# A hybrid scan and mixture-of-experts layer on one core: rows sorted by expert on chip, expert results put back by products

## Chip, core and metric

The kernel runs on one core of one Trainium2 chip. The metric is the device time of one execution in microseconds, as the median of three runs.

## What is computed

One layer of a diffusion trunk on 384 tokens (128 prompt, 256 sample) of width 1024, all in float32: a modulated norm, a wide projection, two groups of scans (Mamba-2 and RWKV-7), the output product, and then the part that the change is about, a mixture of 32 experts of which each token uses two:

```python
h = rmsnorm(x, norm2_w) * (1.0 + scale2) + shift2
grp_logits = (t @ w_grp) + b_grp                  # 4 groups, the best one is taken
exp_logits = (t @ w_exp) + b_exp                  # 8 experts in it, the best two
gates = sum(one_hot(expert_id) * top_w)           # two weights of each token
hid = silu(einsum('td,edf->tef', t, w_gate)) * einsum('td,edf->tef', t, w_up)
out = einsum('tef,efd->td', hid * gates, w_down)  # D = 1024, D_EXPERT = 256
x = x + gate2 * out
```

A last norm follows, and the outputs are stored.

## The kernel before, in words

The kernel is written engine by engine, with semaphores set by hand; each engine runs its list in order. `ps` is PSUM with 8 banks of 512 columns; `P` = 128, `NTILE` = 3 token tiles, `T` = 384, `KT` = 8 channel tiles.

**First pair.** While TensorE runs the 27 projection tiles (`project`, L1641, in a loop over t), VectorE mixes each tile as it comes (`mix`, L2306) and prepares the arrays of the first pair of RWKV heads between them: part 4 of `prep_dve` (L926, L927) behind the mix of tile 24, part 5 (L931, L932) behind that of tile 25. TensorE transposes their result (L494) behind the projection of tile 25. POOL clears two stretches of a ring (L1545) behind `proj_read` of the last tile.

**Router.** After the mix product (L1876), VectorE adds the three tiles of x1, ScalarE computes their roots, TensorE transposes all three (L1888), VectorE makes `hT` out of it in 16 pieces (L2484), one product of 36 rows gives the logits (L1893), they are transposed back (L1897), and VectorE picks the experts (from L2503) and hands the assignments to TensorE for the ranks in each expert (L1908, L1911). `keep_warm` (L453) puts small matmuls between.

**Groups.** Each expert has a chunk of `CH` = 64 slots, and a group is two chunks, so 16 groups (`NG`), and one to five overflow groups for experts with more than 64 tokens; with these inputs there is one. For group n VectorE builds a 0/1 matrix `pick` (`select`, L1253 to L1265), TensorE gathers the tokens of the group by 24 matmuls with it (`rows_T`, L1218), VectorE copies them (L1272), and TensorE forms gate and up for both experts at once in two column tiles of 64 (`gate_up`, L1229). ScalarE applies silu, VectorE multiplies, TensorE transposes the hidden rows (`hidden_T`, L1238), VectorE copies (L1284), TensorE forms the down product in column tiles (`down_proj`, L1249), and ScalarE copies it (`expert_out`, L1296) and stores it to DRAM (`y_dram`). On TensorE the order of a group is gate/up of n, hidden transposes of n-1, gathering of n+1, down product of n-1:

```python
gate_up(pe, n, b)
if not first:
    hidden_T(pe, n - 1, 1 - b)
rows_T(pe, n + 1)
if not first:
    down_proj(pe, n - 1, 1 - b)
```

SP loads the weights of two groups ahead (`expert_gate_up`, `expert_down`), 6.29 MB for a group.

**End.** POOL gathers for each token the two rows of `y_dram` that are its own (six indirect DMAs, L1582), ScalarE and VectorE weigh and add them (`x2_tile`, L2586 to L2596), and the last norm and the stores follow (L2601, L1448).

Of the kernel before, what the change touches and what calls it, by code (L numbers as in the profile page):

```python
# [15 lines left out]
ds = bass.ds  # L16
# [86 lines left out]
def program(nc, a, out):  # L103
    ctx = ExitStack()
    with ctx:
# [853 lines left out]
        def round_dve(dve, c, b, prev, nxt):  # L959
# [97 lines left out]
            if prev:  # L1057
# [9 lines left out]
        xgT = at(um_f, 2048, 2, KT, P)  # L1067
        yg = at(um_f, 4096, 2, D)
        hs = at(um_f, 6144, 2, DE)
        hid = at(um_f, 6656, 2, DE)  # L1070
        hidT = at(um_f, 7168, 2, 2, P)
        wr = at(um_f, 7680, KT, 36)
        h2sq = at(um_f, 4096, D)
        mx_f = mixm[:, :, :].rearrange("p i t -> p (i t)")
        fnw = at(mx_f, 0, D)
        ymoe = misc[:, 10240:10240 + D]
        lg = at(scratch, 0, NTILE, 36)
        lgT = scratch[0:36, 2048:2048 + T]
# [10 lines left out]
        irow = at(scratch, 880, P)  # L1089
        srel = at(scratch, 872, 2, NTILE)  # L1090
        pick = at(scratch, 2432, NTILE, P)
        erow = at(scratch, 1011, 32)
        down = at(scratch, 1043, 36)
        brt = at(scratch, 1079, 36)
# [7 lines left out]
        slots_i = wdt_f[:, 0:6].bitcast(U32)  # L1102
        gcol = wdt_f[:, 112:144].rearrange("p (t v) -> p t v", v=2)
        meta_i = wdt_f[:, 150:151 + N_CHUNKS + N_OV].bitcast(I32)
        zrow = vrows[0:16, 0, :]
        cmb = at(um_f, 0, 2, 2, D)
        rconst = sem("zeros_and_router_constants")
# [4 lines left out]
               [[(at(misc, 3072, 2, 4, DE), 0, 4), (at(um_f, 0, 2, 4, DE), 4, 4)],  # L1112
                [(at(mx_f, D, 2, 4, DE), 0, 4), (at(misc, 10240, 2, 4, DE), 4, 4)]]]
        wdn = [[at(h, 4096, 2, D) for h in half], [at(hT_flat, 0, 2, D), at(um_f, 7968, 2, D)]]
        GU_LOADS, DN_LOADS = (4, 8), 2
# [8 lines left out]
        y_dram = nc.dram_tensor("expert_rows", [N_GROUPS * P, D], F32).ap()  # L1124
# [16 lines left out]
        lgT_ok = sem("expert_major_logits_ready")  # L1141
# [3 lines left out]
        slots_ok = sem("slots_ready")  # L1145
        meta_ok = sem("loop_table_ready")
        zero_ok = sem("overflow_rows_zeroed")
        sel_c = sem("selection_steps")
        sel_ok = sem("selection_ready")
        gu_in = [sem("gate_up_loaded_0"), sem("gate_up_loaded_1")]  # L1150
        dn_in = [sem("down_loaded_0"), sem("down_loaded_1")]
        yst = [sem("expert_rows_stored_0"), sem("expert_rows_stored_1")]
        xt_ps = sem("rows_transposed")
        xt_rd = sem("rows_ready")
# [7 lines left out]
        comb = [sem("combined_rows_0"), sem("combined_rows_1")]  # L1162
        moe_ok = sem("moe_summed")
        cmb_w = sem("first_expert_row_weighed")
# [46 lines left out]
        def rows_T(pe, n):  # L1211

            pe.wait_ge(sel_ok, n + 1)
            if late(n, 1):
                pe.wait_ge(xt_rd, n)
            for k in range(KT):
# [3 lines left out]
            mm.then_inc(xt_ps, 1)  # L1220

        def gate_up(pe, n, b, before=2):
            pe.wait_ge(xt_rd, n + 1)
            if late(n, 2):
                pe.wait_ge(hid_ok, n - (before - 1))
            for k in range(KT):
                for x in range(2):
                    h = slice(CH * x, CH * x + CH)
                    mm = pe.matmul(ps[h, 2 + b, :], xgT[:, b, k, h], gate_up_tile(b, x, k), start=(k == 0),  # L1229
                                   stop=(k == KT - 1), tile_position=(0, CH * x), skip_group_check=True)  # L1230
            mm.then_inc(gu_ps, 1)
# [21 lines left out]
        def select(dve, n):  # L1253

            if late(n, 1):
                dve.tensor_scalar(srel, srel, float(P), None, ALU.subtract).then_inc(sel_c, 1)
            else:
                dve.tensor_copy(srel, slots).then_inc(sel_c, 1)
            dve.wait_ge(sel_c, n * 2 + 1)
            for j in range(NTILE):  # L1260
                ins = dve.tensor_scalar(pick[:, j, :], irow, srel[:, 0, j:j + 1], None, ALU.is_equal)
            ins.then_inc(sel_c, 1)
            dve.wait_ge(sel_c, n * 2 + 2)
            for j in range(NTILE):
                ins = dve.scalar_tensor_tensor(pick[:, j, :], irow, srel[:, 1, j:j + 1], pick[:, j, :], ALU.is_equal, ALU.add)  # L1265
# [1369 lines left out]
```

## Time and profile before

| what | us |
|---|---|
| median of 3 runs (1238.7 to 1243.1) | 1241.46 |
| the profiled execution's own time | 1237.3 |
| its span | 1235.4 |
| TensorE matmul busy, share of the span | 1128.7 (91%) |
| VectorE busy | 562.6 (46%) |
| ScalarE busy | 333.8 (27%) |
| GpSimd busy | 139.4 (11%) |
| mean granted TensorE clock | 0.955 |

All durations of the trace are from the one profiled execution. Its rows name engines PE (TensorE matmul), PEld (weight load), DVE (VectorE), ACT (ScalarE), POOL (GpSimd), SPq (the sync engine's queue), and source lines as L1229. PEclk is the granted TensorE clock as a share of 2.4 GHz; 0.50 is 1.2 GHz. In a chain, each piece is the work that released the next one; in a timeline, the brackets tell how long the engine sat idle and what ended it.

### The profile page before, as it was taken

The numbers are of one execution on the slowest core, as the hardware profiler recorded it, in microseconds if no ns is written. First come the engines' busy times: TensorE is split into PE (matmuls) and PEld (weight loads), VectorE is DVE, ScalarE is ACT, GpSimd is POOL, SyncE is SP. The second block draws the span as 40 slices with busy tenths as digits, with TensorE's granted clock in tenths as the row PEclk, the third lists the DMA queues.
The fourth block names the chain that finished last, engine by engine and source line by source line (L and its number), as shares of the span: only waits on it lengthen the run. The fifth ranks groups of instructions, "written<-read, shape, count | busy, mean of one in ns | idle before, by whom it ended". The sixth has DMA issues, their size and how long they took to land.

```text
span 1235.4 us, 34632 instructions
## 1 busy us (share of the span) xinstructions
PE 1128.7 (91%) x15658; PEld 722.3 (58%) x15658; DVE 562.6 (46%) x1305; ACT 333.8 (27%) x701; POOL 139.4 (11%) x186
## 2 busy tenths in 40 slices
PE   5899889999999779999999999789989999999990
PEld 3555336677765466656666566575575555555540
DVE  0355102567676465756657666531662212222214
ACT  2022101322234244535445345321220000000012
POOL 6000001032103030303203023000000000000002
PEclk9899988999999889999999999879999999999995
DMA  9533555331218201110211201203286999999874
GB/s 333 205 136 136 204 204 160 103 86 68 69 30 129 45 4 33 56 55 27 73 43 44 64 28 37 105 3 103 71 360 235 408 416 416 416 416 415 334 287 159
DMA packets 83665, 201.28 MB, mean 163 GB/s; under 512 B 12484, under 2 KB 27079, under 8 KB 78919
## 3 DMA queue, kind: packets, MB, share of 16 engines
q1 hardware_dynamic: 79392, 186.97, 42.2%
q10 hardware_dynamic: 3271, 9.08, 1.8%
q0 software_dynamic: 864, 3.15, 0.8%
q8 instruction: 116, 1.90, 0.6%
q14 instruction: 22, 0.18, 0.0%
HBM read 183.97 MB, written 15.20 MB: 161 GB/s over the span
## 4 chain that ended last, share of the span: by engine, by line
PE 86%; DVE 4%; DMA 3%; issue 3%; ACT 3%; POOL 0%; POOLq 0%; SPq 0%; ACTq 0%; DVEq 0%; PEldq 0%
PE ps L1641 16%; PE ps L1229 10%; PE ps L1218 7%; PE ps L568 5%; PE ps L1249 5%; PE ps L616 4%; PE ps L1684 4%; PE ps L1876 3%; PE ps L550 2%; PE ps L1764 2%; PE ps L1780 2%; PE ps L482 2%; PE ps L600 1%; DMA ring_a<-in_w_in 1%; PE ps L1603 1%
## 5 line engine op out<-in xcount | busy, mean ns | idle before, releaser
L1641 PE MATMUL ps<-hT,ring_a 128*128 128x384 f32 x624 | 215.7, 501 | 3.4 <-DVE hT L2224 2.5
L1641 PEld LDWEIGHTS ps<-hT,ring_a 128*128 128x128 f32 x624 | 119.7, 196 | 85.1 <-issue 9.5
L1218 PE MATMUL ps<-scratch,misc 128*128 128x128 f32 x864 | 99.7, 275 | 1.3 <-DVE scratch L1265 1.3
L1218 PEld LDWEIGHTS ps<-scratch,misc 128*128 128x128 f32 x864 | 97.9, 192 | 3.1 <-issue 3.1
L2306 DVE SCALAR_TENSOR_TENSOR um_a<-ps,mum,um_a 128x252 f32<-128x252 f32 (+1 forms) x162 | 57.3, 410 | 73.2 <-ACT um_a L2023 72.2
L568 PEld LDWEIGHTS ps<-ring_a 32*32 32x32 f32 x6144 | 63.0, 106 | 42.8 <-issue 30.2
L568 PE MATMUL ps<-ring_a 32*32 32x32 f32 x6144 | 71.6, 195 | 14.9 <-issue 14.9
L1229 PE MATMUL ps<-ring_a,um_a 128*64 128x512 f32 x288 | 63.4, 593 | 1.6 <-DVE um_a L1272 1.4
L1284 DVE COPY um_a<-ps 128x256 f32<-128x256 f32 x17 | 7.2, 425 | 125.5 <-PE ps L1238 125.5
L1508 POOL TENSOR_TENSOR mixm<-tri,la 128x512 f32<-128x512 f32 x24 | 28.4, 1207 | 271.8 <-DVE la L2276 187.2
L1229 PE MATMUL ps<-misc,um_a 128*64 128x512 f32 x128 | 56.3, 592 | 1.4 <-DVE um_a L1272 1.4
L1296 ACT ACTIVATE um_a<-ps 128x1024 f32<-128x1024 f32 x17 | 17.4, 1026 | 143.0 <-PE ps L1249 143.0
L616 PE MATMUL ps<-ring_a,mixm 128*128 128x512 f32 x96 | 54.0, 645 | 0.0
L1272 DVE COPY um_a<-ps 128x1024 f32<-128x1024 f32 x17 | 20.8, 1225 | 71.5 <-PE ps L1218 70.7
L1684 PE MATMUL ps<-ring_a,hT 128*128 128x512 f32 x96 | 46.8, 648 | 6.9 <-DMA ring_a<-in_w_in 6.9
L2023 ACT ACTIVATE um_a<-ps,mum 128x384 f32<-128x384 f32 x27 | 15.7, 582 | 130.6 <-PE ps L1641 130.6
L1582 POOL DMA_INDIRECT um_a<-expert_rows,wdt x6 | 6.7, 1122 | 367.9 <-DMA expert_rows<-um_a 361.9
L1229 PEld LDWEIGHTS ps<-ring_a,um_a 128*64 128x64 f32 x288 | 21.1, 137 | 42.0 <-issue 42.0
L999 DVE COPY_PREDICATED ring_a<-lvl,ps 128x128 f32<-128x128 int32 x96 | 26.7, 278 | 39.4 <-PE ps L568 39.1
L1603 PE MATMUL ps<-ring_a,cond 128*32 128x512 f32 x192 | 28.2, 712 | 12.7 <-DMA ring_a<-in_w_ada 10.3
L1290 ACT ACTIVATE um_a<-ps 128x256 f32<-128x256 f32 x17 | 6.5, 385 | 122.0 <-PE ps L1229 122.0
L1684 PEld LDWEIGHTS ps<-ring_a,hT 128*128 128x128 f32 x96 | 19.6, 208 | 31.1 <-issue 24.0
(422 smaller groups left out, 2009.0 us busy)
## 6 DMA issues: line engine op xcount, KB each, us to landing
ring_a<-in_w_ada SPq DMA_DIRECT2D x12, 2048.0 KB, 12.5
ring_a<-in_w_in SPq DMA_DIRECT2D x11, 2048.0 KB, 9.1
ring_a<-in_moe_w_gate SPq DMA_DIRECT2D x18, 1024.0 KB, 9.4
ring_a<-in_moe_w_up SPq DMA_DIRECT2D x18, 1024.0 KB, 11.6
ring_a<-in_moe_w_down SPq DMA_DIRECT2D x18, 1024.0 KB, 11.8
ring_a<-in_w_out SPq DMA_DIRECT2D x48, 256.0 KB, 2.7
expert_rows<-um_a ACTq DMA_DIRECT2D x17, 512.0 KB, 7.0
misc<-in_moe_w_gate SPq DMA_DIRECT2D x16, 512.0 KB, 9.2
```

Of the source, the lines that this page charges most:

```text
L568: mm = pe.matmul(ps[r, 2 * s + 1, m:m + 32], lhs[r, h, d, :], rhs[r, h, d, :], start=True, stop=True, tile_position=(32 * q, 32 * q), skip ...
L616: pe.matmul(ps[:, 7, :], mixm[:, k, P * (r // 2):P * (r // 2) + P], mamba_w[n % RING], start=(k == 0), stop=(k == KT - 1)).then_inc(half_p ...
L999: dve.copy_predicated(xc[s], level_mask(l, False), ps[:, 2 * s + 1, P:2 * P].rearrange("p (h d q) -> p h d q", h=2, d=2)).then_inc(x_ok, 1)
L1218: mm = pe.matmul(ps[:, k // 4, P * (k % 4):P * (k % 4) + P], h2[:, j, P * k:P * k + P], pick[:, j, :], start=(j == 0), stop=(j == NTILE - 1))
L1229: mm = pe.matmul(ps[h, 2 + b, :], xgT[:, b, k, h], gate_up_tile(b, x, k), start=(k == 0), stop=(k == KT - 1), tile_position=(0, CH * x), s ...
L1249: mm = pe.matmul(ps[h, 5 + c, :], hidT[:, b, k, h], wdn[b][x][:, k, BLK * c:BLK * c + BLK], start=(k == 0), stop=(k == 1), tile_position=( ...
L1508: ins = pool.tensor_tensor(lam[:, j, 4 * d:4 * d + 4, :], tri[:, 2 - 2 * d, :].unsqueeze(1).to_broadcast([P, 4, P]), la[:, j, h:h + 4].uns ...
L1603: mm = pe.matmul(ps[32 * q:32 * q + 32, ada_bank(i), :], cond[:, 2 * q + k2, :], slot(n)[:, 2 * q + k2, :], start=(k2 == 0), stop=(k2 == 1 ...
L1641: mm = pe.matmul(ps[:, t % 4 if isinstance(t, int) else t, 0:T], slot(n)[:, k, P * c:P * c + P], hT[:, k, :], start=(k == 0), stop=(k == K ...
L1684: mm = pe.matmul(ps[:, i % 4, :], hT[:, k, P * j:P * j + P], slot(n)[:, k, :], start=(k == 0), stop=(k == KT - 1))
L1876: mm = pe.matmul(ps[:, 2 * j + c, :], um_a[:, k, P * j:P * j + P], wout_tile(k)[:, BLK * c:BLK * c + BLK], start=(k == 0), stop=(k == KT - 1))
L2306: ins = dve.scalar_tensor_tensor(dst, src, mum[:, m, t:t + 1], dst, ALU.mult, ALU.add)
```

## The change

It does four things. (1) The first pair's parts 4 and 5 on VectorE move one tile ahead, and POOL's memsets wait for the projection in place of its reading. (2) The router goes by token tiles: transposes, halves of `hT` on VectorE and ScalarE, and logits for each tile, with the tokens on the rows of the result; its weights are loaded ahead of x. (3) `rows_T` in each group goes. Once, before the first group, `sort_rows` puts all 768 token rows in the order of their experts, channel-major in `sortT`, by products with a 0/1 matrix `pk`; for each group VectorE reads two offsets into registers and copies two stretches of 64 columns (`expert_columns`). (4) The expert rows are no longer stored to DRAM and gathered. A matrix `put` that holds each token's weight at its slot is built for each group (`put_matrix`), and six matmuls (`put_unit`: three token tiles by two halves) give the group's share of all 384 tokens, which VectorE adds up in `acc2` (`add_units`). In the loop the units of group n-2 stand between the gate/up products of group n. `acc2` is weighed and added to x1 ahead of the overflow group, whose units are added one by one. TensorE's loop is written out instead of run by registers; one gate/up weight block is in three pieces instead of two.

The diff, cut to its core ("..." marks what is left out):

```diff
@@ L1211, rows gathered per group -> rows sorted once; units
-        def rows_T(pe, n):
...
+        def sort_rows(pe):
+            for i in range(2 * KT):
+                blk, k = i // KT, i % KT
+                if k == 0:
+                    pe.wait_ge(pk_ok, blk + 1)
+                if i >= 6:
+                    pe.wait_ge(srt_sb, i - 5)
                 for j in range(NTILE):
-                    mm = pe.matmul(ps[:, k // 4, P * (k % 4):P * (k % 4) + P], h2[:, j, P * k:P * k + P], pick[:, j, :],
+                    mm = pe.matmul(ps[:, i % 6, 0:T], h2[:, j, P * k:P * k + P], pk[blk][j],
                                    start=(j == 0), stop=(j == NTILE - 1))
+                mm.then_inc(srt_ps, 1)
+        def slot_rows(pe):
+            pe.wait_ge(slots_ok, 1)
+            for i, cols in enumerate((slots[:, 0], slots[:, 1], wcol[:, 0], wcol[:, 1])):
+                for j in range(NTILE):
+                    mm = pe.matmul(ps[:, (0, 1, 5, 6)[i], P * j:P * j + P], cols[:, j:j + 1].to_broadcast([P, P]), ident[:, :],
+                                   start=True, stop=True)
+            mm.then_inc(row_ps, 1)
+        UNIT_BANK = (0, 1, 7)
+        def put_unit(pe, m, b, u):
+            if u == 0:
+                pe.wait_ge(put_ok, m + 1)
+                pe.wait_ge(yg_ok, m + 1)
+            if late(m * 6 + u, 3):
+                pe.wait_ge(unit_rd, m * 6 + (u - 2))
+            pe.matmul(ps[:, UNIT_BANK[u % 3], :], put[b][:, P * (u // 2):P * (u // 2) + P],
+                      yg[:, BLK * (u % 2):BLK * (u % 2) + BLK], start=True, stop=True).then_inc(unit_ps, 1)
@@ gate_up: the units of group n - 2 behind k = 1 to 6
-            pe.wait_ge(xt_rd, n + 1)
+            pe.wait_ge(x_in, n + 1)
...
+                if behind is not None and 1 <= k < 7:
+                    put_unit(pe, behind, behind % 2, k - 1)
@@ L1253, VectorE's helpers: select and rows_copy go
+        def expert_columns(dve, n, b, chunks, before=2):
+            rows = [dve.value_load(off_i[0:1, ds(c, 1)], min_val=0, max_val=2 * T) for c in chunks]
             if late(n, 2):
                 dve.wait_ge(gu_ps, n - (before - 1))
+            dve.tensor_copy(xgT[b][:, :, 0:CH], sortT[:, :, ds(rows[0], CH)])
+            dve.tensor_copy(xgT[b][:, :, CH:P], sortT[:, :, ds(rows[1], CH)]).then_inc(x_in, 1)
+        def put_matrix(dve, m, b):
...
+            dve.scalar_tensor_tensor(put[b], slot_row[:, 0, :], prow[:, 0:1], w_row[:, 0, :], ALU.is_equal, ALU.mult)
+            dve.scalar_tensor_tensor(put_k, slot_row[:, 1, :], prow[:, 0:1], w_row[:, 1, :], ALU.is_equal, ALU.mult).then_inc(put_c, 1)
+            dve.wait_ge(put_c, m * 2 + 2)
+            dve.tensor_tensor(put[b], put[b], put_k, ALU.add).then_inc(put_ok, 1)
+        def add_units(dve, m):
+            for u in range(6):
+                dst, src = acc2[:, u // 2, BLK * (u % 2):BLK * (u % 2) + BLK], ps[:, UNIT_BANK[u % 3], :]
+                dve.wait_ge(unit_ps, m * 6 + u + 1)
+                if m:
+                    dve.wait_ge(unit_rd, m * 6 + u - 5)
+                    dve.tensor_tensor(dst, dst, src, ALU.add).then_inc(unit_rd, 1)
...
@@ L1292, expert_out: no store to DRAM
+            if late(m, 1):
+                act.wait_ge(unit_ps, m * 6)
+            act.activation(yg.rearrange("p (c n) -> p c n", c=2), ps[:, 5:7, :], ACT.Copy).then_inc(yg_ok, 1)
-            act.dma_start(y_dram[ds(m * P, P), :], yg[:, b, :]).then_inc(yst[b], 16)
@@ POOL: memsets of the first pair; the gathers go
-            pool.wait_ge(proj_read, XBC + 6 + RT)
+            pool.wait_ge(proj, XBC + 6 + RT)
...
-                    pool.indirect_dma_start(out=cmb[:, j % 2, k, :], out_offset=None, in_=y_dram,
@@ L1882, TensorE: router by tiles, then the loop, unrolled
+            x1_T(0)
+            keep_warm(pe, ps[:, 6, 0:P], 4)
+            x1_T(1)
+            keep_warm(pe, ps[:, 6, 0:P], 4)
+            pe.wait_ge(late_in, 16 * 4)
+            logits(0)
+            logits(1)
+            h2_back(0)
+            x1_T(2)
+            keep_warm(pe, ps[:, 6, 0:P], 8)
+            logits(2).then_inc(lg_ps, 1)
+            h2_back(1)
+            h2_back(2)
...
+            sort_rows(pe)
+            for n in range(NG):
+                i, b = n // 2, n % 2
+                pe.wait_ge(gu_in[b], (i + 1) * (16 * GU_LOADS[b]))
+                gate_up(pe, n, b, behind=n - 2 if n >= 2 else None)
+                if n == 0:
+                    slot_rows(pe)
+                else:
+                    hidden_T(pe, n - 1, 1 - b)
+                    pe.wait_ge(dn_in[1 - b], (n + 1) // 2 * (16 * DN_LOADS))
+                    if n == 1:
+                        pe.wait_ge(row_ok, 1)
+                    down_proj(pe, n - 1, 1 - b)
             hidden_T(pe, NG - 1, 1)
+            for u in range(6):
+                put_unit(pe, NG - 2, 0, u)
             pe.wait_ge(dn_in[1], NG // 2 * (16 * DN_LOADS))
             down_proj(pe, NG - 1, 1)
+            for u in range(6):
+                put_unit(pe, NG - 1, 1, u)
             with pe.Fori(0, overflow(pe)) as o:
...
-                rows_T(pe, o + (NG + 1))
+                for u in range(6):
+                    put_unit(pe, o + NG, 0, u)
@@ L2432, VectorE: the first pair's parts one tile sooner
-                elif t == 24:
+                elif t == 23:
                     dve.wait_ge(yT_ps, 8)
                     prep_dve(dve, -1, 0, pc, 4)
-                elif t == 25:
+                elif t == 24:
                     prep_dve(dve, -1, 0, pc, 5)
@@ VectorE: the sorting matrix
+            for blk in range(2):
+                for j in range(NTILE):
+                    ins = dve.tensor_scalar(pk[blk][j], iw[:, blk, :], pos[:, 0, j:j + 1], None, ALU.is_equal)
+                chain.do(ins)
+                for j in range(NTILE):
+                    ins = dve.scalar_tensor_tensor(pk[blk][j], iw[:, blk, :], pos[:, 1, j:j + 1], pk[blk][j], ALU.is_equal, ALU.add)
+                ins.then_inc(pk_ok, 1)
@@ VectorE: the loop and what follows
+            for n in range(1, NG):
+                if n >= 2:
+                    add_units(dve, n - 2)
+                hidden_copy(dve, n - 1, 1 - n % 2)
+                hidden_mul(dve, n, n % 2)
+                if n < NG - 1:
+                    expert_columns(dve, n + 1, 1 - n % 2, (2 * n + 2, 2 * n + 3))
+                put_matrix(dve, n - 1, 1 - n % 2)
+            hidden_copy(dve, NG - 1, 1)
+            put_matrix(dve, NG - 1, 1)
+            add_units(dve, NG - 2)
+            add_units(dve, NG - 1)
...
+            for j in range(NTILE):
+                ins = dve.tensor_tensor(acc2[:, j, :], acc2[:, j, :], g2[:, min(j, 1), :], ALU.mult)
+            chain.do(ins)
+            for j in range(NTILE):
+                ins = dve.tensor_tensor(x1[:, j, :], x1[:, j, :], acc2[:, j, :], ALU.add)
+            chain.do(ins)
             with dve.Fori(0, overflow(dve)) as o:
+                expert_columns(dve, o + NG, 0, (o * 2 + 2 * NG, o * 2 + (2 * NG + 1)), before=1)
+                put_matrix(dve, o + NG, 0)
                 hidden_mul(dve, o + NG, 0, before=1)
                 hidden_copy(dve, o + NG, 0, before=1)
+                for u in range(6):
...
+                    dve.tensor_tensor(acc2[:, j, c], ps[:, UNIT_BANK[u % 3], :], g2[:, min(j, 1), c], ALU.mult).then_inc(unit_rd, 1)
+                    dve.wait_ge(unit_rd, (o + NG) * 6 + u + 1)
+                    dve.tensor_tensor(x1[:, j, c], x1[:, j, c], acc2[:, j, c], ALU.add).then_inc(put_add, 1)
```

## Rows read from the trace of the kernel before

**Rows 1.** Page, part 4: share of the chain that ended last, by engine.
```profile
PE 86%; DVE 4%; DMA 3%; issue 3%; ACT 3%; POOL 0%; POOLq 0%; SPq 0%; ACTq 0%; DVEq 0%; PEldq 0%
```

**Rows 2.** Chain, third group and one steady group: start us, us, engine, tile, line, count.
```profile
957.18 6.87 PE ps L1229 x32
...
1005.72 6.87 PE ps L1229 x32
1012.59 0.37 PE ps L1238 x2
1012.95 5.36 PE ps L1218 x48
1018.31 3.58 PE ps L1249 x16
```

**Rows 3.** Windows: busy us (instructions) of PE, PEld, DVE, ACT, POOL; PEclk, DMA share, GB/s.
```profile
850.00:860.00 10.00, 10.00 (x38) 5.53 (x37) 0.00 (x0) 1.02 (x1) 0.00 (x0) 1.00 0.00 0
...
1090.00:1100.00 10.00, 10.00 (x72) 6.84 (x70) 1.50 (x3) 0.39 (x1) 0.00 (x0) 1.00 1.03 418
...
1208.00:1212.00 4.00, 0.00 (x0) 0.00 (x0) 0.00 (x0) 0.00 (x0) 3.09 (x4) 0.68 0.64 184
```

**Rows 4.** Timeline around the last projections of the first pair: start us, us, engine, line.
```profile
400.80 10.59 PE L1641 MATMUL ps<-hT,ring_a 128*128 128x384 f32 x32 [0.90 <-DVE um_a L2306]
...
415.21 1.08 PE L494 MATMUL ps<-ident,misc 128*128 128x128 f32 x4 [3.82 <-DVE misc L931]
...
416.09 7.73 PE L1641 MATMUL ps<-hT,ring_a 128*128 128x384 f32 x16
```

**Rows 5.** Timeline from the mix product's end to the ranks.
```profile
885.64 5.52 PE L453 MATMUL ps<-ident 128*128 128x128 f32 x48
...
904.17 0.27 DVE L2503 TENSOR_TENSOR scratch<-ps,scratch 128x108 f32<-128x108 f32 x1 [6.39 <-PE ps L1897]
...
909.89 0.41 PE L1908 MATMUL ps<-scratch,tri 128*128 128x32 f32 x2
...
911.25 0.83 PE L1911 MATMUL ps<-scratch,ones 128*128 128x32 f32 x6
```

**Rows 6.** Timeline, passes of 384 columns: ScalarE out of PSUM, VectorE in SBUF.
```profile
394.77 0.49 ACT L780 ACTIVATE pair<-ps 128x384 f32<-128x384 f32 x1
...
919.97 0.55 DVE L2557 TENSOR_TENSOR scratch<-scratch 128x384 f32<-128x384 f32 x1
```

**Rows 7.** Timeline, VectorE at the entry of the overflow loop.
```profile
1185.32 1.23 DVE L1272 COPY um_a<-ps 128x1024 f32<-128x1024 f32 x1 [0.79 <-issue]
```

**Rows 8.** Chain, mix product, matmuls of 512 columns.
```profile
868.63 17.17 PE ps L1876 x40
```

**Rows 9.** Chain, the overflow group: hidden transposes and down products.
```profile
1196.83 0.44 PE ps L1238 x2
...
1197.83 3.67 PE ps L1249 x16
```

**Rows 10.** Timeline of one group, edges between tiled and full-array products.
```profile
1011.99 0.59 PE L1229 MATMUL ps<-um_a 128*64 128x512 f32 x1
...
1012.52 0.44 PE L1238 MATMUL ps<-ident,um_a 128*128 128x128 f32 x2
...
1012.79 5.52 PE L1218 MATMUL ps<-scratch,misc 128*128 128x128 f32 x48
...
1018.24 3.65 PE L1249 MATMUL ps<-ring_a,um_a 128*64 128x512 f32 x16
...
1021.73 7.04 PE L1229 MATMUL ps<-ring_a,um_a 128*64 128x512 f32 x32
```

**Rows 11.** Timeline of the end: last square on ScalarE, last table load, last scale.
```profile
1220.51 1.28 ACT L2183 ACT_TABLE_LOAD   x1
...
1229.35 1.06 ACT L2181 ACTIVATE um_a<-misc 128x1024 f32<-128x1024 f32 x1 [2.60 <-DVE misc L2596]
...
1231.06 1.28 DVE L2601 SCALAR_TENSOR_TENSOR misc<-misc,mstat,mixm 128x1024 f32<-128x1024 f32 x1
```

More of the change, by code:

```diff
@@ L1251, in down_proj @@
             mm.then_inc(dn_ps, 1)
[L1253 to L1265, printed above, removed]
-            ins.then_inc(sel_ok, 1)
@@ L2520, in _ @@
             dve.tensor_tensor(s3[:, 4, :], s3[:, 3, :], s3[:, 2, :], ALU.subtract).then_inc(rt_dve, 1)
+            dve.wait_ge(lg_ps, 2)
+            n_e = ps[:, 7, 96:128]
+            rank = ps[:, 7, 0:96].rearrange("p (j e) -> p j e", j=NTILE)
+            chain.do(dve.tensor_tensor_scan(n_to, ones[:, 0:32], n_e, 0.0, ALU.mult, ALU.add))
+            chain.do(dve.tensor_tensor(first, n_to, n_e, ALU.subtract))
+            chain.do(dve.tensor_tensor(slot_v, rank, row(first, 32), ALU.add))
+            for k in range(2):
+                chain.do(dve.tensor_tensor(tmp, slot_v, oh[:, k], ALU.mult))
+                chain.do(dve.tensor_reduce(pos[:, k, :], tmp, AX.X, ALU.add))
+            for blk in range(2):
[5 more added lines that the diff above has]
+                ins.then_inc(pk_ok, 1)
+            dve.tensor_copy(off_i[:, 0:NE], first).then_inc(meta_ok, 1)
             dve.wait_ge(rt_act, 1)
@@ L2558, in _ @@
             chain.do(dve.tensor_tensor(mq, mq, mq2, ALU.mult))
+            chain.do(dve.scalar_tensor_tensor(off_m, cnt[:, 2, :], -float(CH), first, ALU.mult, ALU.add))
+            chain.do(dve.tensor_tensor(mq2, mq, by_chunk(off_m), ALU.mult))
+            chain.do(dve.tensor_reduce(off_x, mq2, AX.X, ALU.add))
+            chain.do(dve.scalar_tensor_tensor(off_x, erow[:, 0:n_ov], float(CH), off_x, ALU.mult, ALU.add))
+            chain.do(dve.tensor_reduce(s_q, mq, AX.X, ALU.max))
+            chain.do(dve.scalar_tensor_tensor(off_x, s_q, float(CH), off_x, ALU.mult, ALU.add))
+            dve.tensor_copy(off_i[:, NE:N_CHUNKS], off_x)
             chain.do(dve.tensor_tensor(mq, mq, by_chunk(erow), ALU.mult))
@@ L2568, in _ @@
             dve.tensor_copy(meta_i[:, :], meta).then_inc(meta_ok, 1)
[L2570 to L2574 removed]
+            dve.wait_ge(meta_ok, 2)
+            dve.wait_ge(rconst, 2)
+            dve.wait_ge(srt_sb, 2 * KT)
+            expert_columns(dve, 0, 0, (0, 1))
+            expert_columns(dve, 1, 1, (2, 3))
+            dve.wait_ge(row_ps, 1)
+            for i in range(2):
+                dve.tensor_copy(slot_row[:, i, :], ps[:, i, 0:T])
+                ins = dve.tensor_copy(w_row[:, i, :], ps[:, 5 + i, 0:T])
```

318 lines of the change are left out of this document (142 added, 176 removed).

## The prediction

> **What bounds the kernel now.** Read the chain of waits on the page first: TensorE carries 86% of it [rows 1]. Then the chain through the expert groups: one group is 6.87 + 0.37 + 5.36 + 3.58 = 16.18 us of gate/up products, hidden transposes, row gathering (`rows_T`) and down products, with nothing between them, and the pattern stands 14 times, from 957.18 to 1183.7 [rows 2]. The windows show the transfers close beside it: DMA share 1.03 at 418 GB/s [rows 3]. A group reads 6.29 MB and stores 0.52 MB, so 6.81/16.18 = 421 GB/s: TensorE sets the pace and the transfers just keep up. So only TensorE's work in a group counts in the loop; outside it, the waits do.
>
> The parts are costed in order of time, against the profiled execution: 1235.4 us span, 1237.3 us time.
>
> **First pair, -6.** TensorE stood idle 3.82 us for VectorE's L931, which came behind the mix of tile 25; the next 16 matmuls then took 7.73 us, where 32 take 10.59, so 5.3 is their price at full clock, and the difference is 2.4 [rows 4]. One tile earlier, L931 stands behind the mix of tile 24 and ends about when that of tile 25 began, so TensorE finds it done. Gain 3.8 + 2.4 = 6.2; ends: nothing (another input is late in its place) and 6.7 (the transposes too run at full clock). I take 6. POOL's memsets behind `proj` instead of `proj_read`: nothing, VectorE's own chain to L2442 releases the same products. The router's four loads move ahead of x's two on SP: nothing, the transfers stand still from 850 to 860 and VectorE, which x feeds, works in none of these 10 us [rows 3].
>
> **From the mix product to the third group, +12.5.** The product ends at 885.8 in both; before, the router began at 904.17 [rows 5]. By tiles: VectorE adds the last x1 tile as before (two passes of 1.23, to 888.4), a root and the first half-tile follow on ScalarE, so `logits(0)` can start near 891.0. From there TensorE runs in order 80 small instructions (logits 3x16, transposes 8+8, warm 16) at 0.12 each (48 took 5.52 [rows 5]), 9.6 us: 900.6, a gain of 3.6. To the assignments 5.7 and the ranks 2.2 as before [rows 5]: 908.5. New on VectorE: seven small steps (about 1.9) and the first block of the sorting matrix, six passes of 384 columns; one took 0.55 [rows 6], and compares should be somewhat faster: 2.9. At 913.3 TensorE starts `sort_rows`: 2 x 8 x 3 matmuls of 384 columns, each two instructions in float32 as in `project`, 96 x 0.331 [rows 4] = 31.8 us, all of it bare, since the first group needs all 16 results; ScalarE's copies (0.49 [rows 6]) hide but the last. End 945.6. Then `expert_columns`: two register loads and two copies of 512 elements. Before, one load with the loop's entry kept VectorE idle 0.79 us [rows 7]; I take 0.8 each, and 0.5 per copy (ends 0.4 and 0.7: no row copies within the chip at this size). First gate/up at 948.4; it takes 7.1, then slot rows 24 x 0.112 = 2.7, gate/up 6.9, transposes with their wait 1.1, down 3.5: third group at 969.7 against 957.2.
>
> **Fourteen groups, +26.2.** `rows_T` goes (5.36). Six put units come: each one float32 matmul of 512 columns, two instructions at 17.17/40 = 0.429 [rows 8], 5.15 together. That alone would gain 0.2. Two things are added. (a) The hidden transposes now stand directly ahead of the down products, with nothing to cover VectorE's copy between. The overflow group of before already runs so: transposes at 1196.83, down at 1197.83 [rows 9]. 1.00 where the steady group pays 0.37: +0.6. (b) A unit uses the whole array, gate/up and down use it as two column tiles of 64. Tiled pairs follow each other at 0.43; behind the last pair (1011.99) the full-array transpose starts 0.53 later, so 0.10 is lost; from the first of the 48 gathers (1012.79) to the first tiled pair (1018.24) are 5.45 against 5.36 in the chain, 0.09 lost, and its eight pairs need 3.49 against 3.44, 0.05 [rows 10]. A round trip costs 0.24 us, six stand in every group: 1.44 us.
> The Trainium skill (TensorEngine Tiling (Array Packing), Key Properties) says that changing the tiling mode, not just the tile, drains TensorE. It speaks against the interleaving; if the drain is what the recorded 0.59 us of a matmul has over its 0.43 spacing, 0.16 each way, the sum by it would be 14 x 6 x 0.08 = 7 us longer; my sum goes by the spacing in the rows.
> New group: 6.87 + 5.15 + 1.44 + 0.10 + 1.00 + 3.49 = 18.05, +1.87, times 14 = 26.2. The switch may cost 0 to 0.32, that is -20 to +7. What hides: VectorE adds the units, six of about 0.7 (half and a little of 1.23 for 1024 elements [rows 7]), while they come every 1.9 us, so three banks do; ScalarE's copy of the down result ends 1.1 us behind it, the first unit comes at 1.7. `expert_out` now waits for the units of the group before, which are long done, and behind it on ScalarE only the next silu stands. Columns of the next group: behind the transposes 0.9 (copy, multiply) + 1.6 + 1.0 = 3.5 us, against 4.4 until TensorE asks; if that cover is gone each us costs 14. Transfers fall to 6.29/18.05 = 348 GB/s; the two more weight pieces per odd group cost SP 0.9 us of issue in its idle time.
>
> **End of the loop to the last down product, +25.5.** Before 1183.7 to 1201.5 = 17.8 [rows 2, 9]. After, in a row: units of group 14 with a wait of 1.2 for ScalarE's copy and 5.15, down 3.6, copy 1.2, units of group 15 5.15, last add 0.8: 17.1. Then VectorE weighs and adds acc2 in six passes of 1024, 6 x 1.23 = 7.4, and only behind them come loop entry 0.8, loads 1.6, copies 1.0 and a hand-over 0.1 for the overflow group, which always runs once: 28.0. TensorE has idled 11 us by then. Before, its last matmul ended near 1207, and the granted clock of 1208 to 1212 was 0.68 [rows 3]: the group begins at half clock, and as in rows 4 some 2.5 us are added to 7.1. Then silu and product 1.0, transposes 1.1, down 3.6: 43.3.
>
> **Tail, -12.6.** Before 1201.5 to 1235.4 = 33.9: store, six gathers from DRAM, sums, norm. After: copy and first unit 2.3; VectorE multiplies, then adds, each of six half rows, 12 x 0.7 = 8.5; square to scale 1.7 and a table load 1.3 for the first tile, 1.5 for each other; from the last scale (1231.06) to the end 4.3 [rows 11]: 21.3 with 0.2 of hand-overs.
>
> Sum: -6 + 12.5 + 26.2 + 25.5 - 12.6 = +45.6, so 1282.9. The median of the runs shown, 1241.5, lies 4.2 above the profiled execution; with it 1287.1. I put 1285.
>
> **Rivals.** (1) *Switches cost nothing* where a unit of 0.86 us follows, since its second weights load early. For: the losses of rows 10 are at small matmuls. Against: they stand at both kinds of edge. -20: 1265. Chance 0.2.
> (2) *VectorE becomes the bound.* Its place is `expert_columns`; it decides from 0.9 us more than my 3.5. For: 0.79 idle for one load [rows 7], and no row shows such a copy. At 1 us late per group +14: 1299. Chance 0.15. The Trainium skill (DMA: Bandwidth & Descriptors, Latency and other measured facts) gives some 600 ns as the least for a `tensor_load`; two would be 1.2 us by it, and the columns would not be late.
> (3) *Faster than before.* The one mechanism big enough: put units run beside the tiled products, TensorE taking both in little more than the time of one. The units are 84 in the loop at 1.10 and 18 behind it at 0.86, 108 us; the gain begins once one costs under about 0.63 us, less than its own two passes. Free units leave the groups at the transfers' floor (6.29/421 = 14.9 us, -17 in place of +26) and take 10 off the end: 1232. Against: rows 8 show 0.429 for each pass with the array to itself, and a steady group has no idle TensorE time. Chance 0.05.
> (4) *The early preparation does not do what it says*, another input is late: +6, 1291. Chance 0.1.
> The forecast has 0.5.
>
> **Numbers.** Under about 0.3% (4 us) a measurement of this kernel can't tell a change from none. Rival 3 and a little of 1 with other errors on the same side are faster or same: faster 0.05, same 0.02, slower 0.93. Range 1258 to 1304: free switches and 7 us more that I overcharged, to late columns and a half clock behind the sort as well.
>
> **What would show it.** Groups of 18.05 us in the chain, put units between tiled pairs; `sort_rows` as 31 us of TensorE; TensorE idle about 11 us before the overflow group; no 3.8 us idle before the transposes near 411. Wrong if a group is near 16.6 (free switches), if VectorE's columns release gate/up, or if the time falls below 1258.

## The result, and the profile after

The changed kernel takes 1296.2 us (median of 4 runs, 1289.4 to 1300.9), the kernel before 1240.1 in the same comparison: ratio 1.046, 95% interval [1.0423, 1.0497]. Forecast were 1285, a range of 1258 to 1304, and slower with a chance of 0.93. The profiled execution of after took 1300.9 us (span 1299.2), 4.7 more than its median; that of before lies 2.8 below its own. So the spans differ by 63.8 us, the medians by 56.

The page of the changed kernel, busy times (part 1) and the chain by engine (part 4), which stands at 86% for TensorE in [rows 1]:

```profile
PE 1191.5 (92%) x15131; PEld 684.8 (53%) x15131; DVE 631.7 (49%) x1395; ACT 342.5 (26%) x725; POOL 134.5 (10%) x181
...
PE 88%; DVE 4%; issue 3%; DMA 3%; ACT 1%; DVEq 0%; SPq 0%; PEldq 0%; ACTq 0%
```

TensorE is the bound before and after, and the span grew by 63.8 us while its busy time grew by 62.8. Where they came, cut at the same four points in both profiled executions:

| stretch | before | after | difference | forecast |
|---|---|---|---|---|
| start to the mix product's end | 885.8 | 882.3 | -3.5 | -6 |
| to the third group's gate/up | 71.4 | 91.3 | +19.9 | +12.5 |
| fourteen groups | 226.5 | 261.7 | +35.2 | +26.2 |
| end of the loop to the last down product | 17.8 | 42.8 | +25.0 | +25.5 |
| tail | 33.9 | 21.1 | -12.8 | -12.6 |

One steady group in the chain of waits (start us, us, engine, line, count), to be held against [rows 2]:

```profile
973.59 1.72 PE ps L1266 x8
975.31 1.06 PE ps L1256 x2
976.36 1.01 PE ps L1266 x4
977.37 1.06 PE ps L1256 x2
...
987.70 0.37 PE ps L1278 x2
988.07 0.56 issue
988.63 3.65 PE ps L1289 x16
992.28 0.82 PE ps L1266 x3
```

L1256 is a put unit, L1266 gate/up. The group is 992.28 - 973.59 = 18.69 us. A unit and the four gate/up instructions behind it take 2.07; the passes alone are 2 x 0.429 + 4 x 0.215 = 1.72. So one round trip between the two tilings costs 0.35 us, where 0.24 were forecast. The timeline shows its edges (start us, us, engine, line, shapes):

```profile
1217.71 0.59 PE L1266 MATMUL ps<-mixm,hT 128*64 128x512 f32 x1
1218.23 1.12 PE L1256 MATMUL ps<-mixm,scratch 128*128 128x512 f32 x2
1219.29 0.64 PE L1266 MATMUL ps<-misc,hT 128*64 128x512 f32 x1
...
1219.77 0.59 PE L1266 MATMUL ps<-misc,hT 128*64 128x512 f32 x1
```

Tiled pairs follow each other at 0.43. Into the unit it is 0.52 (0.10 lost, as in [rows 10]); the unit's two passes are worth 0.86 and the next tiled pair comes 1.06 behind its start (0.20 lost, where [rows 10] gave 0.09 behind a small matmul); the next pair comes 0.48 later (0.05 lost). Every product has a weight load (PEld) on record, and these loads tell where the time goes:

```profile
1217.24 0.14 PEld L1266 LDWEIGHTS ps<-misc,hT 128*64 128x64 f32 x1 [0.26 <-issue]
...
1218.23 0.30 PEld L1256 LDWEIGHTS ps<-mixm,scratch 128*128 128x128 f32 x2 [0.81 <-issue]
1219.28 0.13 PEld L1266 LDWEIGHTS ps<-misc,hT 128*64 128x64 f32 x1 [0.76 <-issue]
```

Between tiled products the weights are loaded one product ahead: the load of 1217.24 belongs to the product that starts at 1217.67. At a change they are not: both loads of the unit start with its first product at 1218.23, and the load of the tile behind it starts at 1219.28.

Behind the mix product, TensorE's timeline (in brackets the idle time before, and what ended it) and the windows (busy us of PE, PEld, DVE, ACT, POOL; PEclk, DMA share, GB/s) of the changed kernel:

```profile
884.74 1.06 PE L453 MATMUL ps<-ident 128*128 128x128 f32 x8
887.84 6.24 PE L1929 MATMUL ps<-um_a,hT 128*128 128x36 f32 x32 [2.04 <-ACT hT L2196]
...
907.51 0.41 PE L1956 MATMUL ps<-scratch,tri 128*128 128x32 f32 x2 [0.85 <-DVE scratch L2573]
```
```profile
888.00:892.00 4.00, 4.00 (x24) 4.00 (x23) 0.20 (x1) 1.09 (x4) 0.00 (x0) 0.59 1.02 428
892.00:896.00 4.00, 4.00 (x20) 4.00 (x21) 0.00 (x0) 0.00 (x0) 0.00 (x0) 0.50 1.00 411
896.00:900.00 4.00, 4.00 (x26) 4.00 (x25) 1.36 (x4) 2.43 (x5) 0.00 (x0) 0.63 1.02 410
```

The logits of two tiles (L1929) took 6.24 us at half clock, and the ranks' products start 25.4 us behind the first instruction that follows the mix product, where before it was 24.3. VectorE's passes for the sorting matrix and its last table entry, and the sort in the chain:

```profile
913.14 1.67 DVE L2590 SCALAR_TENSOR_TENSOR um_a<-rst,scratch,um_a 128x384 f32<-128x384 f32 x3
...
929.42 0.19 DVE L2643 CAST wdt<-scratch 128x51 int32<-128x51 f32 x1
950.91 0.43 DVE L1298 COPY states<-um_a 128x512 f32 x1 [21.30 <-issue]
```
```profile
910.06 7.60 PE ps L453 x56
917.66 30.98 PE ps L1234 x96
```

The first block of the sorting matrix is ready at 914.8, but the sort starts at 917.7: released by the 56 warming instructions ahead of it. The sort is 30.98 us, and VectorE's last table entry is done at 929.6. TensorE has nothing beside the sort, and the chain goes through all of it. But the table stands ahead of the first columns in VectorE's list, so a shorter sort would save at most the 19.0 us from 929.6 to 948.6; the first 12 run beside the table.

The end, in the chain. TensorE stands still from 1252 to 1263:

```profile
1246.58 5.40 PE ps L1256 x12
...
1252.80 3.51 DVE misc L2672 x3
1256.36 1.10 issue
1257.47 2.36 DVE misc L2675 x2
...
1263.14 9.29 PE ps L1266 x32
...
1274.43 3.67 PE ps L1289 x16
```

### The profile page after: what moved, and what is told of

It reads as the page before. It is cut to its first block, busy times and chain, and to the rows that moved or that the text cites. A ratio compares the mean times of both kernels' runs of the same rounds, so it can differ in the third digit from the quotient of the medians.

```text
span 1299.2 us, 33869 instructions
## 1 busy us (share of the span) xinstructions
PE 1191.5 (92%) x15131; PEld 684.8 (53%) x15131; DVE 631.7 (49%) x1395; ACT 342.5 (26%) x725; POOL 134.5 (10%) x181
## 4 chain that ended last, share of the span: by engine, by line
PE 88%; DVE 4%; issue 3%; DMA 3%; ACT 1%; DVEq 0%; SPq 0%; PEldq 0%; ACTq 0%
PE ps L1677 15%; PE ps L1266 10%; PE ps L1256 8%; PE ps L568 5%; PE ps L1289 5%; PE ps L616 4%; PE ps L1720 4%; PE ps L1912 3%; PE ps L1234 2%; PE ps L550 2%; PE ps L1800 2%; PE ps L1816 2%; PE ps L482 1%; PE ps L600 1%; DMA ring_a<-in_w_in 1%
## 5 line engine op out<-in xcount | busy, mean ns | idle before, releaser
L1321 DVE TENSOR_TENSOR misc<-misc,ps 128x512 f32<-128x512 f32 x90 | 61.8, 688 | 133.1 <-PE ps L1256 133.0
L1266 PE MATMUL ps<-ring_a,states 128*64 128x512 f32 x288 | 75.1, 624 | 14.5 <-DVE states L1299 14.5
L1266 PE MATMUL ps<-misc,hT 128*64 128x512 f32 x128 | 65.3, 609 | 0.0
L1256 PE MATMUL ps<-mixm,stw 128*128 128x512 f32 x108 | 58.3, 635 | 2.2 <-ACT mixm L1347 1.4
L1256 PE MATMUL ps<-mixm,scratch 128*128 128x512 f32 x96 | 52.7, 639 | 1.2 <-issue 1.2
L1266 PEld LDWEIGHTS ps<-ring_a,states 128*64 128x64 f32 x288 | 18.5, 139 | 64.2 <-issue 64.2
L1639 PE MATMUL ps<-ring_a,cond 128*32 128x512 f32 x192 | 28.1, 710 | 12.6 <-DMA ring_a<-in_w_ada 10.1
L1256 PEld LDWEIGHTS ps<-mixm,stw 128*128 128x128 f32 x108 | 16.8, 188 | 42.5 <-DVE misc L1321 24.8
L971 DVE TENSOR_TENSOR ring_a<-ps,tri 128x512 f32<-128x512 f32 x48 | 30.6, 679 | 16.3 <-PE ps L550 16.3
L1347 ACT ACTIVATE mixm<-ps 128x1024 f32<-128x1024 f32 x17 | 17.4, 1024 | 77.3 <-PE ps L1289 77.3
## 6 DMA issues: line engine op xcount, KB each, us to landing
ring_a<-in_w_ada SPq DMA_DIRECT2D x12, 2048.0 KB, 12.6
```

Of the source, the lines that this page charges most:

```text
L971: ins = dve.tensor_tensor(gk[p][:, h].rearrange("p d a t -> p (d a t)"), src, tri[:, :, :].rearrange("p i t -> p (i t)"), ALU.mult)
L1256: pe.matmul(ps[:, UNIT_BANK[u % 3], :], put[b][:, P * (u // 2):P * (u // 2) + P], yg[:, BLK * (u % 2):BLK * (u % 2) + BLK], start=True, st ...
L1266: mm = pe.matmul(ps[h, 2 + b, :], xgT[b][:, k, h], gate_up_tile(b, x, k), start=(k == 0), stop=(k == KT - 1), tile_position=(0, CH * x), s ...
L1321: dve.tensor_tensor(dst, dst, src, ALU.add).then_inc(unit_rd, 1)
```

## Experiments

Each comparison has its own runs of the kernel before (medians 1237.4, 1237.4 and 1241.4 in the three), so the ratios are what is to be compared; that of after is 1.046. "After" and "before" name the kernel that was edited.

**e1 and e2: the switches, and the cover of VectorE's copy.** e1 edits after:

```diff
-                gate_up(pe, n, b, behind=n - 2 if n >= 2 else None)
+                gate_up(pe, n, b)
+                if n >= 2:
+                    for u in range(6):
+                        put_unit(pe, n - 2, b, u)
```

e2 puts the six units one step later, and VectorE adds them last in a group:

```diff
                     hidden_T(pe, n - 1, 1 - b)
+                    if n >= 2:
+                        for u in range(6):
+                            put_unit(pe, n - 2, b, u)
                     pe.wait_ge(dn_in[1 - b], (n + 1) // 2 * (16 * DN_LOADS))
```

> The changed kernel with the six put units as one block behind the gate/up products instead of between them; nothing else differs. Theory A (switches between tiled and full-array products cost 0.35 us each way and back, six in a group, as the changed kernel's trace reads): a group falls from 18.69 to about 17.2 us (minus 2.0, plus up to 0.5 because VectorE adds the last unit before it copies the hidden rows), so -21 us, about 1275, ratio to the kernel before 1.028. Theory B (the units cost time because VectorE and the three banks pace them, not because of switches): the block is paced by VectorE's 0.69 us adds all the more, the group stays within 0.3 us of 18.7, about 1296, ratio 1.045.

> The changed kernel with the six put units as one block between the hidden transposes and the down products, and VectorE's order changed so that the columns and the put matrix come ahead of the hidden copy and the adds behind it. Theory A: no switches and no uncovered copy, a group is 6.87 + 0.37 + 5.2 + 3.6 = 16.0 to 16.1 us, 2.6 less than in the changed kernel, fourteen times -37: about 1259, ratio 1.016; still slower than before, because the sort (31 us) and the overflow group stand. Theory B (the adds of VectorE pace the block): 17 us or more, above 1272.

Measured: e1 1272.3 us, ratio 1.0259 [1.0211, 1.0307]; e2 1260.8, 1.0197 [1.0143, 1.0251]. A group of e1, then one of e2, in their chains:

```profile
1084.55 5.35 PE ps L1256 x12
1089.90 0.22 PE ps L1278 x2
1090.12 0.94 issue
1091.06 3.65 PE ps L1289 x16
```
```profile
1084.98 6.87 PE ps L1266 x32
1091.84 0.37 PE ps L1278 x2
1092.21 5.15 PE ps L1256 x12
```

Both came out as Theory A said (expected 1.028 and 1.016). A group of e1 is 6.87 + 5.35 + 0.22 + 0.94 + 3.65 = 17.03, 1.66 less than 18.69. A group of after has seven round trips, six for the units and one for the hidden transposes, and e1 has one. Six at 0.35 are 2.1; 0.38 of it are lost again, because VectorE adds the last unit before it copies the hidden rows (0.94 between transposes and down product in place of 0.56). In e2 the units stand over VectorE's copy, the 0.94 go, and a group is 6.87 + 0.37 + 5.15 + 3.58 = 15.97, 0.2 less than before's 16.18. With e10, which takes away the six round trips alone (below, 16.61), the 2.51 us that a group lost divide so: 2.08 are the round trips, 0.64 the open copy (16.61 - 15.97), and the exchange of gathering for units gains 0.21, as forecast.

**e4: the same loss without any unit.** Before, with its gathering in five pieces between gate/up products:

```diff
+                if mixed is not None and 2 <= k < 7:
+                    rows_piece(pe, mixed, ((0,), (1,), (2,), (3,), (4, 5))[k - 2])
```

> The kernel before with ten of the sixteen eighths moved: of the gathering of a group's rows, six of eight channel tiles go in five pieces between the tiled gate/up products, the last two stay between the hidden transposes and the down products, so the hidden copy is still covered. No work is added, only five round trips between tiled and full-array products in each of 15 groups. If a round trip costs 0.35 us whatever the matmul's length: +1.75 a group, +26 us, 1266, ratio 1.021. If it costs the 0.24 us that the edges of 128-column matmuls showed before, and 0.35 only behind matmuls of 512 columns: +1.2 a group, +18 us, ratio 1.0145. If free: within 2 us.

Measured: 1261.2 us, 1.0185 [1.0136, 1.0233]. In its chain (L1229 are six gathering instructions, 0.67 at their pace, L1241 four of gate/up, 0.86 at theirs):

```profile
1108.12 0.87 PE ps L1229 x6
1108.99 1.01 PE ps L1241 x4
1110.00 0.87 PE ps L1229 x6
```

A piece and the gate/up behind it take 1.88 where the passes are worth 1.53: again 0.35 for a round trip, with matmuls of 128 columns as with those of 512. The group is 17.91, 1.73 above before for five of them. The interval of the time covers both what 0.35 and what 0.24 would give (1.021 and 1.0145); the chain tells them apart.

**e10: units in gate/up's own tiling.** After, in the same place:

```diff
-            pe.matmul(ps[:, UNIT_BANK[u % 3], :], put[b][:, P * (u // 2):P * (u // 2) + P],
-                      yg[:, BLK * (u % 2):BLK * (u % 2) + BLK], start=True, stop=True).then_inc(unit_ps, 1)
+            for x in range(2):
+                h = slice(CH * x, CH * x + CH)
+                mm = pe.matmul(ps[h, UNIT_BANK[u % 3], :], put[b][:, P * (u // 2) + CH * x:P * (u // 2) + CH * x + CH],
+                               yg[:, BLK * (u % 2):BLK * (u % 2) + BLK], start=True, stop=True,
+                               tile_position=(0, CH * x), skip_group_check=True)
+            mm.then_inc(unit_ps, 1)
```

> The changed kernel with each put unit written as two column tiles of 64, in the same tiling as gate/up, and in the same place; nothing else differs. Theory A (what costs 0.35 us per round trip is the change between tiled and full-array products, and two tiles of 64 columns side by side take the time of one of 128): a unit takes 0.86 us between the gate/up products, the group falls from 18.69 to 16.6, 14 x 2.1 = 29 us, 1296.2 becomes 1267, ratio 1.0235. Rival B (the loss belongs to the unit itself: its weights, its own bank, the break in the accumulation): the group stays at 18.3 to 18.7, 1291 to 1296, ratio 1.043 to 1.046.

Measured: 1274.3 us, 1.0271 [1.0208, 1.0334]; expected 1.0235. By the ratios that is 23 us less than after, by the spans (1270.1) 29.1, as 14 x 2.08 gives. In its chain, L1258 is the unit, now four instructions:

```profile
1074.26 1.72 PE ps L1270 x8
1075.98 0.86 PE ps L1258 x4
1076.84 0.86 PE ps L1270 x4
...
1087.21 3.65 PE ps L1293 x16
1090.87 1.72 PE ps L1270 x8
```

The group is 16.61 as Theory A said: same units, same place, same order, and the loss is gone. It belongs to the change of tiling, not to the unit. Here the weight loads stand ahead of their products again (the load for the unit of 1075.78 starts at 1075.39).

**e6: is the sort bare?** After, with part of the second block's sum left out, so that its sorted rows are incomplete:

```diff
-                for j in range(NTILE):
+                for j in range(NTILE if blk == 0 else 1):
```

> The changed kernel with two of the three token tiles left out of the sum for the second block of 384 sorted rows (that block is then not what the reference needs; 32 of the 96 instructions of sort_rows are gone). Theory A (the sort stands bare on TensorE, 0.323 us for each instruction): -10.3 us, 1296.2 becomes 1285.9, ratio 1.038; the third group starts 10.3 us earlier in the profile, measured from the sort's first instruction. Rival B (ScalarE's copies of 0.49 to 0.55 or VectorE's table of chunks set the start of the first group, the sort only fills the time): less than 3 us. In the profile after, VectorE's last table entry ends at 929.6 and the sort at 948.6, which speaks for A.

Measured: 1282.8 us, 1.0374 [1.0322, 1.0426]; expected 1.038. From the sort's first instruction to the first gate/up it is 24.2 us in its profile (907.07 to 931.23), and 34.5 in that of after (917.50 to 951.98): 10.3 less, so all 32 instructions that went were bare. They are a third of the sort; for the rest the table (above) sets the bound of 19 us.

**e5: the sum ahead of the overflow group.** e2, with the unit sums alone left ahead of the overflow group:

```diff
-            for j in range(NTILE):
-                ins = dve.tensor_tensor(acc2[:, j, :], acc2[:, j, :], g2[:, min(j, 1), :], ALU.mult)
-            chain.do(ins)
-            for j in range(NTILE):
-                ins = dve.tensor_tensor(x1[:, j, :], x1[:, j, :], acc2[:, j, :], ALU.add)
-            chain.do(ins)
             with dve.Fori(0, overflow(dve)) as o:
...
-                    dve.tensor_tensor(acc2[:, j, c], ps[:, UNIT_BANK[u % 3], :], g2[:, min(j, 1), c], ALU.mult).then_inc(unit_rd, 1)
+                    dve.tensor_tensor(acc2[:, j, c], acc2[:, j, c], ps[:, UNIT_BANK[u % 3], :], ALU.add).then_inc(unit_rd, 1)
...
+            for j in range(NTILE):
+                chain.do(dve.tensor_tensor(acc2[:, j, :], acc2[:, j, :], g2[:, min(j, 1), :], ALU.mult))
+                dve.tensor_tensor(x1[:, j, :], x1[:, j, :], acc2[:, j, :], ALU.add).then_inc(x1_ok, 1)
```

> The kernel of e2 with the last sum rearranged: the two unit sums of the last groups stand alone before the overflow group (the six passes of 1024 elements of VectorE, L2675 and L2678, go from there), in the overflow loop each unit is only added to acc2, and acc2 is weighed and added to x1 behind the loop, tile by tile, with the square of a tile right behind its sum. Theory A (end of the loop, as forecast: those passes stood bare in front of expert_columns): -7.4 before the overflow group, some -1.5 because TensorE's idle stretch of 11 us shrinks to under 5 and the gate/up of the overflow group (8.57 us in e2, 6.87 at full clock) keeps its clock, +0.8 in the tail, where six halves take 5 us instead of 8 but six passes of 1.23 follow. e2 1260.8 becomes about 1252.7, ratio to the kernel before 1.013. Rival B (something else releases the overflow group, its weights or the loop's entry with its register loads): 1258 to 1261, ratio 1.018.

Measured: 1251.5 us, 1.0102 [1.0056, 1.0148], 9.3 less than e2. The passes were bare (Theory A). But one part of it was wrong: the idle stretch fell to 4 us and the clock still did not hold. The chain, and a window:

```profile
1205.84 5.40 PE ps L1256 x12
...
1215.33 9.71 PE ps L1266 x32
```
```profile
1217.00:1220.00 3.00, 3.00 (x10) 0.97 (x8) 0.04 (x1) 0.00 (x0) 0.00 (x0) 0.50 0.00 0
```

The overflow group's gate/up takes 9.71 us behind 4.1 us of idle, more than the 8.57 of e2 behind 11.

**e3: the first pair's part alone.** Before, with these lines of the change and nothing else:

```diff
-            pool.wait_ge(proj_read, XBC + 6 + RT)
+            pool.wait_ge(proj, XBC + 6 + RT)
...
-                elif t == 24:
+                elif t == 23:
                     dve.wait_ge(yT_ps, 8)
                     prep_dve(dve, -1, 0, pc, 4)
-                elif t == 25:
+                elif t == 24:
                     prep_dve(dve, -1, 0, pc, 5)
```

> The kernel before with the first pair's part of the change alone. Theory A: the first small products of the first round start 6.7 us sooner, as in the changed kernel; some of it may be lost to the clock in the rounds, so -3 to -7 us, ratio 0.995 to 0.998. Rival: what the changed kernel's trace gained there is lost again by the mix product (it had 3.5 left of 6.7), and nothing measurable is left, ratio 0.999 to 1.001.

Measured over 12 runs: 1231.3 us, 0.9952 [0.9927, 0.9977]. This part of the change is a gain of its own. The point where the mix product ends also tells it: it lies at 885.6 and 886.8 in the profiles of before and e4, and between 873.6 and 886.5 in the ten profiles of kernels with this part, 880.3 on the mean. Between the means that is 5.9 sooner, though two profiles against ten with such a spread would be weak evidence alone. The spread of 13 us over the same code is why the profile of after shows 3.5 and that of e3 12; part of it goes with the clock (from 430 to 860 it was 0.96 in e6, 0.93 in e9).

**e7 and e8: the router.** e7 is after with more warming matmuls where TensorE had idled for 2.04 us; e8 is before with the first pair's part, the router by tiles and these warming matmuls, and neither sort nor units:

```diff
             x1_T(1)
-            keep_warm(pe, ps[:, 6, 0:P], 4)
+            keep_warm(pe, ps[:, 6, 0:P], 13)
```

> The changed kernel with 13 warming matmuls in place of 4 behind the second tile's transposes in the router, so that TensorE doesn't stand idle for 2.04 us before the first logits. Theory A (the router by tiles lost its forecast gain of 3.6 us because the granted clock fell to 0.50 behind this idle stretch: 888 to 898 in all three profiles of kernels with this router): the logits of two tiles take about 3.7 us instead of 6.2 to 6.8, all up to the assignments comes 4 to 5 us earlier, and mix product's end to assignments falls from 25.2 to about 20.5; 1296.2 becomes 1291.8, ratio 1.042. Rival B (the clock falls because of the small products themselves, with 36 columns, idle or not): the clock row 888 to 898 still reads 0.50, 0 +- 1 us.

> The kernel before with two parts of the change and nothing else: the first pair's parts one tile sooner (as e3) and the router by tiles with its loads ahead of x, with 13 warming matmuls as in e7. Theory A (the forecast gain of the router was right and is only paid back by the clock): from mix product's end to the assignments about 20 us instead of 24.1, so e3's 1231.3 becomes 1227.3, ratio to the kernel before 0.992. Rival B (the router by tiles gains nothing in itself): 1231 to 1232, ratio 0.995.

Measured: e7 1295.7 us, 1.0467 [1.0424, 1.051]; e8 1225.9, 0.9904 [0.9872, 0.9936]. In the profile of e7 the ranks start 22.15 us behind the mix product in place of 25.4, and the two tiles' logits take 3.73:

```profile
884.66 3.07 PE L453 MATMUL ps<-ident 128*128 128x128 f32 x26
887.76 3.73 PE L1929 MATMUL ps<-um_a,hT 128*128 128x36 f32 x32
```
```profile
888.00:892.00 4.00, 4.00 (x37) 4.00 (x37) 0.12 (x1) 1.02 (x3) 0.00 (x0) 0.96 1.01 426
892.00:896.00 4.00, 4.00 (x25) 4.00 (x24) 1.33 (x4) 1.33 (x4) 0.00 (x0) 0.61 0.99 409
```

The stretch is 3.3 us shorter, but the time shows none of it, and Theory A is half right at most: the clock still falls, only later, with TensorE busy all the while. Nor can the 3.3 us be put down to the filled idle time, since e6 keeps it and has the same stretch:

```profile
876.42 1.04 PE L1921 MATMUL ps<-ident,misc 128*128 128x128 f32 x8
...
882.16 4.14 PE L1929 MATMUL ps<-um_a,hT 128*128 128x36 f32 x32 [2.04 <-ACT hT L2196]
...
898.70 0.41 PE L1956 MATMUL ps<-scratch,tri 128*128 128x32 f32 x2 [0.85 <-DVE scratch L2573]
```

The nine profiles with the router by tiles all have such a fall; ranks stand 22.2 and 22.3 behind the product in e7 and e8, and 22.3 (e6), 23.8 (e9) and 25.4 (the other five) where the 2 us of idle are left in. Of the three with the old router, before and e3 have no such fall and 24.3, e4 has one. So with this router the stretch varies by 3 us with the length of the fall. What makes the clock fall there, and for how long, was not settled. e8's own gain over e3, by the ratios, is 0.5%, with intervals that overlap a little; its first gathering starts 31.0 us behind the product, before 34.1. It is the fastest kernel of this study.

**e9: the warming matmuls ahead of the sort.** e5 with half of them:

```diff
-            keep_warm(pe, ps[:, 6, 0:P], 28)
+            keep_warm(pe, ps[:, 6, 0:P], 14)
             pe.wait_ge(h2_ok, 3)
```

> The kernel of e5 with 14 warming matmuls in place of 28 between the ranks and the sort. In e5's profile the sorting matrix is ready at 912.07 and the sort starts at 915.0, released by those 28 (56 instructions, 7.7 us, part of them at half clock); after shows the same, 914.81 and 917.66. Theory A (they are what made this stretch 7.6 us where 4.8 was forecast): the sort starts at the matrix, 4.8 us behind the ranks, -2.9 us, 1251.5 becomes 1248.6, ratio to the kernel before 1.008. Rival B (they pay for themselves, since without them the clock falls and the sort begins at half clock): the sort's first stretch of 16 us takes 2 us or more longer, 1251 to 1253.

Measured: 1256.3 us, 1.0123 [1.0076, 1.0169], not told apart from e5. In the profile the sort starts at 917.69 behind the matrix (ready at 917.56), 4.9 us behind the end of the ranks (912.8), where e5 has 7.7, and it is hardly slower for it (30.98 in e5):

```profile
917.69 31.21 PE ps L1234 x96
```

So the 2.8 us are there in the profile, but the time doesn't show them (the ratio is 0.002 higher, not lower): in this profile the mix product ended at 886.5 us, in e5's at 879.4, and such a spread of the same code hides them.

## Why the prediction was right, and where it was off

The sign and its causes held: a sort that TensorE does ahead of all groups, round trips between tilings, an end that waits for VectorE. 1296 lies in the range, 11 us above the number. The misses did not cancel: the large ones (4.7, 2.8 and 9 us) all made the kernel slower than forecast.

- **First pair, -6:** right. e3 gives 0.9952 of 1237, -5.9 us; in the changed kernel the idle stretch of [rows 4] is gone and the first round starts 6.7 sooner.
- **Mix product to third group, +12.5:** measured +19.9. The step that failed is "TensorE runs in order 80 small instructions at 0.12 each". It priced them at full clock; for the most part they met a clock of 0.50 to 0.63 and took 13.9 us in place of 9.6. The idle 2.04 us ahead of them are no part of this, since they started 5.5 us behind the product where 5.2 were forecast. The assignments came at 25.2 us in place of 20.5 (+4.7), so the router by tiles lost a microsecond here where it was to gain 3.6. The second is "At 913.3 TensorE starts `sort_rows`": the text gave VectorE's preparation 4.8 us and overlooked TensorE's own 56 warming instructions between ranks and sort, 6.3 us at full clock and 7.6 here (+2.8; e9's profile shows it). The sort's "all of it bare" was too strong: at most 19 us of the sort are (e6 shows 10.3), which changes what a shorter sort is worth, but not this sum. The sort (31.8, measured 30.98), the first columns and the first groups came within 0.8 us.
- **Fourteen groups, +26.2:** measured +35.2. All of the difference is the term "A round trip costs 0.24 us": it is 0.35, so 6 x 0.11 x 14 = 9 us. It was read at edges with small matmuls and the way out of a full pass of 512 columns, 0.20 in place of 0.09, stood in no row. The two additions (a) and (b) are shown: e2 takes both away, e1 and e10 the second alone. The Trainium skill (TensorEngine Tiling (Array Packing), Key Properties) says that a change of tiling mode drains TensorE; the estimate given beside it, 0.32 and 7 us more, was the better one, and e10, without a change of mode, loses nothing, which agrees. Whether the array drains or only the weights come late, these traces do not separate.
- **End, +25.5, and tail, -12.6:** +25.0 and -12.8. The idle TensorE, VectorE's passes ahead of the columns and the gate/up at half clock (9.29, forecast 9.6) are all in the chain; e5 takes the passes away and gains 9 us.
- **Rivals.** Free switches: refuted by e1, e4 and e10; the second weights do load early (both loads of the unit stand at 1218.23), but the first do not. VectorE as bound: no group is released by the columns. In the group shown they are done at 990.3, 2.0 us before gate/up. At the overflow group, where they are bare, the two loads took 1.3 us with their register steps (1.6 forecast); the load instruction itself took 0.30, half of the 600 ns that the prediction cites as the least. Units beside the tiled products: a unit costs 1.06 and more with its switch. Early preparation without effect: refuted by e3.

With the measured terms the sum is 1282.9 + 7.4 + 9.0 + 2.5 - 0.5 - 0.2 = 1301.1, and the profiled execution took 1300.9; since the stretches cover the whole span, this must be so, and it shows only where the misses lie. Of these 18 us over the sum 7.5 are the two executions' distances from their medians (4.7 and 2.8), so the medians show some 10.5.

## What to carry to other kernels

Interleaving full-array matmuls with column-tiled ones costs TensorE at each change; put them in one block, or write the small product in the tiling of its neighbours, where two tiles of 64 took the time of one of 128. Work that runs once ahead of a loop that TensorE bounds, as the sort here (31 us of TensorE), must be paid back by the loop, and an exchange that gains 0.2 us a group in sixteen groups can't. Of a change in several parts measure each alone: the two small parts here, with some warming added, make before 1% faster (e8), where the whole change costs 4.6%.

## What the runs showed of the hardware

- A round trip from column tiles of 64 to the full array and back costs 0.35 us of TensorE's time: in after, and in e4 behind matmuls of 128 columns. Weight loads, which stand 0.4 us ahead of their product within one tiling (1217.24 for 1217.67), start only with it at a change (1218.23, 1219.28). With 512 columns 0.10 of it lie on the way in, 0.20 on the way out and 0.05 in the first tiled pair.
- The granted clock fell to 0.50 in stretches in which TensorE was busy without a gap (892 to 895 in e7; in after it fell between 888 and 889, about a microsecond behind 2.04 us of idle, and stayed there with TensorE busy from 889 to 898), each time in a row of small products. Filling the idle time ahead of them did not take the fall away, and a shorter stretch was seen with it (e7, 22.2 us to the ranks) and without it (e6, 22.3).
- The same code up to the mix product ended between 873.6 and 886.5 us in ten profiles. Of changes under 5 us a profile's stretch tells more than the time of four runs.
